# One inference step of an RWKV-7 / mLSTM / retention trunk: where ScalarE decays the sample states of a retention step

## What is computed

```python
def retention_chunkwise(S0, q, k, v):
    ...
    def step(S, inp):
        qc, kc, vc = inp
        s = jnp.einsum('bjhd,bihd->bjih', qc, kc) * mask[None]
        o = jnp.einsum('bjih,bihe->bjhe', s, vc) + jnp.einsum('bjhd,bhde->bjhe', qc * q_dec[None, :, :, None], S)
        S = c_dec[None, :, None, None] * S + jnp.einsum('bihd,bihe->bhde', kc * k_dec[None, :, :, None], vc)
        return S, o
```

## Time and profile before

| | |
|---|---|
| median of 3 runs | 2313.78 us (2312.76 to 2318.72) |
| the profiled execution | 2319.36 us, span 2317.6 us |
| mean granted TensorE clock over the span | 0.914 |
| TensorE busy | 2069.7 us, 89% |
| VectorE busy | 1099.0 us, 47% |
| ScalarE busy | 690.4 us, 30% |
| chain that ended last, by engine | PE 76%, DVE 13%, DMA 4%, ACT 4%, issue 3% |

### The profile page before, as it was taken

How to read it: one execution, slowest core, us unless ns; L and a number is a source line. 1 busy time by engine, 2 the same in 40 slices (tenths; PEclk the granted TensorE clock), 3 DMA queues, 4 the chain that set the end, 5 groups by cost and what they waited for, 6 DMA issues and landing times.

```text
span 2317.6 us, 36907 instructions
## 1 busy us (share of the span) xinstructions
PE 2069.7 (89%) x15010; PEld 1876.9 (81%) x15010; DVE 1099.0 (47%) x1631; ACT 690.4 (30%) x963; POOL 80.6 (3%) x90
## 2 busy tenths in 40 slices
PE   8998666967667989999989998999899899999989
PEld 8996556856335779999989996666699889999988
DVE  5662776665463064234335764444563254234234
ACT  3323222222121143223224213322442243223222
POOL 0000110110000100000010000000000100000000
PEclk9998778977655989999999999889899999999999
DMA  5230000002001312222221322443332212222231
GB/s 197 85 99 5 1 0 0 0 0 95 19 1 46 122 61 91 91 91 91 91 100 55 127 91 109 165 172 145 118 112 93 87 55 91 91 91 91 91 100 55
DMA packets 44718, 186.70 MB, mean 81 GB/s; under 512 B 5480, under 2 KB 5992, under 8 KB 39272
## 3 DMA queue, kind: packets, MB, share of 16 engines
q1 hardware_dynamic: 44648, 185.72, 23.3%
HBM read 160.54 MB, written 25.16 MB: 80 GB/s over the span
## 4 chain that ended last, share of the span: by engine, by line
PE 76%; DVE 13%; DMA 4%; ACT 4%; issue 3%; POOL 0%; DVEq 0%; POOLq 0%; SPq 0%; ACTq 0%
PE ps L1965 52%; PE ps L1848 4%; PE ps L726 4%; PE ps L327 3%; DMA h_a<-in_rst 2%; DMA out_rst_o<-h_a 2%; DVE h_a L1735 2%; PE ps L1923 1%; ACT h_a L1794 1%; DVE free L409 1%; PE ps L345 1%; PE ps L1539 1%; PE ps L1522 1%; PE ps L1336 1%; DVE rb L364 1%
## 5 line engine op out<-in xcount | busy, mean ns | idle before, releaser
L1953 DVE TENSOR_TENSOR w_low<-slot,w_high 128x1024 fp32r<-128x1024 f32 x240 | 294.1, 1226 | 500.5 <-ACT w_high L1949 500.5
L1949 ACT ACTIVATE w_high<-slot 128x1024 fp32r<-128x1024 f32 x240 | 254.0, 1060 | 799.8 <-PE ps L1965 769.6
L1965 PE MATMUL ps<-x_high,w_high 128*128 128x260 f32 x1824 | 367.9, 283 | 1.1 <-issue 1.1
L1965 PE MATMUL ps<-x_high,w_low 128*128 128x260 f32 x1824 | 367.6, 283 | 0.0
L1965 PE MATMUL ps<-x_low,w_high 128*128 128x260 f32 x1824 | 367.0, 283 | 0.0
L1965 PE MATMUL ps<-hidden_high,w_low 128*128 128x260 f32 x1536 | 309.5, 283 | 0.0
L1965 PE MATMUL ps<-hidden_high,w_high 128*128 128x260 f32 x1536 | 309.4, 283 | 0.0
L1965 PE MATMUL ps<-hidden_low,w_high 128*128 128x260 f32 x1536 | 309.0, 283 | 0.0
L1965 PEld LDWEIGHTS ps<-x_high,w_high 128*128 128x128 f32 x1824 | 281.7, 189 | 1.8 <-issue 1.5
L1965 PEld LDWEIGHTS ps<-x_high,w_low 128*128 128x128 f32 x1824 | 281.2, 188 | 0.0
L1965 PEld LDWEIGHTS ps<-x_low,w_high 128*128 128x128 f32 x1824 | 280.4, 188 | 0.0
(11 more groups left out here) (588 smaller groups left out, 2608.2 us busy)
## 6 DMA issues: line engine op xcount, KB each, us to landing
slot<-in_w SPq DMA_DIRECT2D x240, 512.0 KB, 3.7
h_a<-in_rst SPq DMA_DIRECT2D x16, 1024.0 KB, 4.9
out_rst_o<-h_a SPq DMA_DIRECT2D x16, 1024.0 KB, 3.9
slot<-in_w SPq DMA_DIRECT2D x2, 2048.0 KB, 10.9
con<-in_con SPq DMA_DIRECT2D x1, 2126.0 KB, 16.5
h_a<-in_x SPq DMA_DIRECT2D x4, 520.0 KB, 5.1
h_a<-in_x SPq DMA_DIRECT2D x1, 2080.0 KB, 12.5
out_y<-h_a SPq DMA_DIRECT2D x8, 260.0 KB
```

The costliest lines, as they stand in the source:

```text
L1949: nc.scalar.activation(wh[c % 2], raw[c % 4], ACT.Copy).then_inc(s_wh, 1)
L1953: nc.vector.tensor_tensor(wl[c % 2], raw[c % 4], wh[c % 2].bitcast(F32), ALU.subtract).then_inc(s_wl, 1)
L1965: mm = pe.matmul(ps[:, 2 * par + hf, 0:HALF], w[c % 2][:, at], y(kt, hf), start=(start and kt == 0 and w is wh and y is x), stop=(stop and ...
```

## The change

ScalarE's decay is called for the step itself, behind the normalised output (L1818) and ahead of the wait for its transposes (L1821), in place of one step ahead in front of the square root. The waits within `decay` and those on its semaphore are the same.

```diff
                 if s:
                     act_high(act, c_q, LEAD + s + 1, 0, (s_tile, t_q + LEAD + s))
-                else:
-                    decay(0)
                 after(ep, "vr")
                 a.activation(vTk[s % 2], ps[:, B_V, :], ACT.Copy).then_inc(*ea.step("vt"))
...
                 if s > 12:
                     act_gate_silu(act, s - 13)
-                if s < STEPS - 1:
-                    decay(s + 1)
                 after(ed, "ag")
                 a.activation(sdev[s % 2], mv[s % 2][:, 1:2], ACT.Sqrt, bias=GN_EPS).then_inc(*ea.step("sd"))
...
                              bias=nmu[s % 2]).then_inc(*ea.step("yn"))
+                decay(s)
                 after(ep, "yt")
```

## The result

The changed kernel takes 2283.07 us, median of 4 runs (2279.46 to 2285.83), against 2313.27 us (2310.55 to 2318.72, 4 runs) of the kernel before: ratio 0.9863, 95% interval 0.9849 to 0.9878. It is 30.2 us faster; 31.2 us had been forecast. The profiled execution of the changed kernel took 2280.58 us, with a span of 2278.8 us. The kernel's lines behind the edit stand two to four numbers lower: the square root is L1810, the normalised output L1814, its transpose L1818, the row choice L1920, the weight pieces L1845.

The account below looks back on a forecast made before the run. Bound: in the retention steps ScalarE's decay waits for its load ahead of the square root, closing a one-step loop. Minus 39.2 us, plus 8.0 us for clock falls, 31.2 us off the 2313.8 us median: 2282.6 us, range 2273 to 2300.

Parts of the forecast that it names:

- What bounded the kernel: Retention steps: update, store, load, decay, root and update form a loop; ScalarE waits 78.1 us for loads.
- The step without the loop, 15.13 us: Retention steps behind step 0: TensorE's own order at 2.4 GHz sets 15.13 us, 39.2 us less over the stage.
- The falls of the clock, 5 of 1.6 us each, 8.0 us: TensorE in the retention steps: drops to 1.2 GHz behind 5 of 15 steps give back 8.0 us.
- The working against the profiled execution, 2288.2 us: Whole kernel: 2319.4 us of the profiled execution, minus 39.2 plus 8.0, before moving to the median.
- The decay at nothing: ScalarE behind the normalisation: the decay ends 0.35 us before it is needed, cost 0, upper bound 31 us.
- The waits: Retention steps: load wait from 78.1 us to under 2, transfers out of the chain, L1735 at 16 x 0.67.
- Table loads: ScalarE, steps 13 to 15: the root's 1.28 us load runs behind the gate's SiLU, same number, cost 0.
- The clock stays high: Rival on TensorE's clock: at most two falls in fifteen, 2274.6 to 2277.8 us; chance 0.20.
- nearly always falls: Rival on TensorE's clock: nine to fifteen falls give back 14.4 to 24.0 us, 2289.0 to 2298.6; chance 0.14.
- The late decay: Rival: VectorE's first value update waits for the decay; slower, 2322 at x = 1.91; chance 0.05, a little late 0.05.
- The loop isn't freed: Rival in the retention steps: the load is still waited for in each step, time stays at 2314; chance 0.06.
- The Trainium skill's price of a throttled clock: Retention stage: throttled time times one minus clock share, 31.1 us, plus 15.5 us waits, 46.6; prediction chose 39.2.

Follow-up runs that it names:

- place: Changed kernel, but the decay stays one step ahead, behind the normalised output instead of before the square root: sixteen steps 250.06 us, whole execution 2281.34 us.
- ownership: Changed kernel, but each step's own decay stands at the old place ahead of the square root: sixteen steps 247.46 us, whole execution 2280.59 us.
- bytes: Kernel before, order untouched; loads from step 2 on and all stores move a quarter of the bytes: sixteen steps 249.55 us, whole execution 2286.12 us.
- the repeated run of the changed kernel: Changed kernel, nothing altered, measured again beside the kernel with both later edits: 2285.64 us, ratio 0.9844, sixteen steps 249.52 us.
- the moved piece alone: Changed kernel with TensorE's eighth weight piece moved in front of the second pair of row choices: 2272.55 us, ratio 0.9803.
- the early split: Changed kernel with the eighth weight piece moved and, in head steps, VectorE's value split ahead of the weight chunk's low part: 2272.24 us, again 2273.77 us.

## Why the prediction was right

- **What bounded the kernel:** right. Three runs, each touching one thing (place, ownership, bytes), give back 32.9 to 35.5 of the 35.5 us of the retention steps. One reading was loose: VectorE's state update doesn't need the standard deviation. It stands behind the reciprocal and the negative mean in VectorE's queue, and so waits with them.
- **The step without the loop, 15.13 us:** measured 15.13 to 15.16 us in all eight steps of the changed kernel behind step 0 that begin no head and have no fall of the clock. Head steps, for which I took the same, are 15.20 us undisturbed, and the last step, which waits for its own sample sums, 15.50 us (both from the repeated run of the changed kernel). Step 0 stayed at 16.65 us.
- **The falls of the clock, 5 of 1.6 us each, 8.0 us:** mis-sized. Behind step 0 the changed kernel's profile has four, behind steps 3, 7, 11 and 15. The sixteen steps are 16.65 + 11 x 15.13 + 3 x 15.20 + 15.50 = 244.2 us without them, so they cost 3.3 us in all. Three lay over the beginning of a head step, where each cost about 0.8 us; some 0.44 us of what is missing lay in TensorE's wait for VectorE's split, 0.14 us in a wait for L1684, the rest is not traced. The fourth runs out behind the end of step 15. The 1.6 us hold where a fall touches no head step (the run above). The prediction had said that low clock inside a wait costs nothing, and then didn't apply it to its own term. In the sixteen steps 35.5 us were gained where the sum had 31.2 us: 4.7 us less for the falls, against that 0.6 us more for the head steps and the last one (and 0.1 us by the ends of the measure).
- **Why the median is so close all the same:** in part by chance. The profiled executions differ by 38.8 us: 35.5 us in the retention steps, 4.3 us ahead of them, in code that didn't change, and 1 us the other way behind them. The 4.3 us come from the input side of layer 0 (matmuls of L1539). The windows of the kernel before, then of the changed kernel:

```profile
212.00:224.00 12.00, 12.00 (x31) 8.65 (x29) 0.00 (x0) 5.05 (x8) 0.00 (x0) 0.54 0.00 0
```

```profile
212.00:224.00 12.00, 6.67 (x28) 4.55 (x27) 0.71 (x2) 9.74 (x13) 0.00 (x0) 0.92 0.00 0
```

  The same matmuls ran at a clock of 0.54 there and 0.92 here, and what follows them started 5.6 us sooner; some of that was lost again near 640 to 690 us. Differences of this size separate the changed kernel's own runs (2279.46 and 2280.58 against 2285.55 and 2285.83). The working against the profiled execution, 2288.2 us, less 4.3 us for the steps, less 4.3 us ahead of them, plus 1 us behind them, is 2280.6 us; it took 2280.58 us.
- **The decay at nothing:** right. Its margin was worked out as 0.35 us and is 0.45 us; the decay starts 0.1 us before the end of the instruction in front of it, which I had not taken off.
- **The waits:** as foretold: ScalarE's for the load gone, the two transfers out of the chain, L1920's wait at 16 x 0.67 us. Table loads cost nothing: VectorE's longest wait for the root is 0.3 us, in steps 13 to 15 too.
- **The rivals:** "The clock stays high" and "nearly always falls" enclose what came; the clock fell behind four steps in which TensorE had no wait longer than 0.67 us, so the lower end, 2274.6 us, did not come. The late decay did not come, but 1.04 us of extra work brought it. "The loop isn't freed" is refuted.
- **The Trainium skill's price of a throttled clock** ("TensorE: Matmul & The Clock Gate", Terms) gives, as an estimate with the clock of 0.97 that the changed kernel showed, 15.5 us of waits + 31.1 us - (1 - 0.97) x 247.2 = 39.2 us for the sixteen steps. They gave 35.5 us, so it overstates a little here. The prediction's reason, low clock inside waits, fits: in the changed kernel the rule counts 7.4 us of low clock, about 1.7 us of it in step 0, where the falls behind step 0 cost 3.3 us by the step sums.

## What to carry to other kernels

In a double-buffered loop look at where the consumer's wait for the load stands in its engine's queue, not only at how many buffers there are: a wait one step early, ahead of something short that others need, turns two steps' room into one. Idle time of an engine says little by itself: 51 us of waiting for a load cost next to nothing and 78 us cost 35, since only the part that outlasts the other work counts. Once such a loop is open, look again at small waits on TensorE: filling 0.67 us per step was worth nothing before and 9 us after, a third of it through the clock (3.3 us, the falls that did not come).

## What the runs showed of the hardware

- TensorE's granted clock fell to 0.50 for about 3.4 us at a time behind steps whose only wait was 0.67 us, and not behind like ones of the same execution; with that wait filled it did not fall in the 15 steps behind step 0, in any of three profiled executions (the moved piece alone, and twice with the early split). That the wait, and not the new order around it, decides this is not shown. With a wait of 1.4 us there were 14 low stretches from the end of step 0 to the end of step 15, three of them twice as long.
- ScalarE's decay of 128 x 2048, in place, takes 1903 to 1909 ns beside VectorE's state update (L1724), and 1895 to 1917 ns in the kernel before, where no decay ran beside it.
- A quarter of the bytes took 2.4 us instead of 3.9 us to store and 3.5 us instead of 4.9 us to load: 768 KB account for 1.5 and 1.4 us. If the rest shrank in proportion (an estimate from these two sizes), some 1.9 us of the store and 3.0 us of the load don't depend on the bytes. What they are was not tested.
